# The first norm by products with diagonal matrices, products on zeros ahead of them, and small loads issued later

## The chip, the cores and the metric

The kernel runs on one core of a Trainium2 chip. The metric is the time of one execution on the device in microseconds (us), median of several runs. A profile of one execution gives what each engine did: TensorE (PE; its weight loads are PEld), VectorE (DVE), ScalarE (ACT), GpSimd (POOL) and SyncE (SP), and the DMA queues.

## The reference, cut to what matters

Three transformer-like blocks work on x, 256 tokens of 1024 features, in float32, with weights of some 176 MB in all. The change lies in the very first steps: the first norm and what it feeds.

```python
def rms_norm(x, g):
    xf = x.astype(jnp.float32)
    y = xf * lax.rsqrt(jnp.mean(xf * xf, axis=-1, keepdims=True) + EPS)
    return (y * g.astype(jnp.float32)).astype(x.dtype)
...
        h = rms_norm(x, norm_mix_pre[i])
        if i % N_MIXERS == 0:
            h = sliding_window_attention(h, attn_w_qkv[j], attn_b_qkv[j], attn_sinks[j],
                                         attn_w_o[j], attn_b_o[j])
...
    qkv = h @ w_qkv + b_qkv
```

## The kernel before

The program is written out by hand: each engine has one instruction stream, and semaphores order the streams. Nothing is rescheduled, so the order in the code is the order on the engine.

The weights come as 336 units of 128 x 1024 float32 (512 KB). SyncE loads them into a ring of six buffers (`raw`): the first six at once, behind x, and each later one when VectorE has made the low half of the unit six before it (`lo_done`). Every matrix product is done in three products of reduced precision: ScalarE copies a unit to its high half (`w_hi`, helper `hi_of`, L151), VectorE subtracts that from the unit for the low half (`w_lo`, `lo_of`, L156), and the activations are split likewise into `a_hi` and `a_lo` (both in the tensor `both`). `hi_to(act, n)` and `lo_to(dve, n)` bring the halves of all units up to n. TensorE then runs high by high, high by low and low by high (L173, L174, L175), eight feature tiles for a unit, 24 products in all.

The activations of the first matrix product are the normed x, with its features on the partitions. x has two tiles of 128 tokens (TT = 2) and eight of 128 features (KT = 8). In the kernel before:

- ScalarE issues the loads of the identity (`ident`, in the table `tab`) and of `cols` (per-feature constants, the gains of all norms among them), squares both tiles of x with a sum (L291), and takes the root for both at once (L296); VectorE computes the mean before it (L304) and the inverse after it (L309).
- VectorE multiplies x by the factor in four pieces of 128 x 512 (`scale_dve`, L320) into `ybuf`.
- TensorE transposes the 16 blocks of `ybuf` (`turn_pe`, L275), each pair of feature tiles signalled when its four blocks are done.
- ScalarE copies each transposed feature tile, times the gain, to the high half (`halves_act`, L332), VectorE makes the low half, times the gain too (`halves_dve`, L337). Both wait for `cols`. VectorE waits for high halves in pairs.
- ScalarE makes the high halves of weight units 0 and 1, and VectorE their low halves, before those of the activations.
- TensorE multiplies units 0 to 3 of the query and key projection (`qk1_pe`); for unit 0 it waits for each low half of the activations.
- Ahead of the transposes TensorE does six products of the identity with itself in three groups (`keep_warm`, L283): one when the identity is there, and one after the sum of each tile.

GpSimd sets `pad` to zero at the very beginning (L2262); the convolutions further on use it. `ps` is the accumulator memory, `st` small statistics, `arena` scratch.

Of the kernel before, what the change touches and what calls it, by code (L numbers as in the profile page):

```python
# [40 lines left out]

WARM_FIRST, WARM = 2, 4
HELD = 4
# [43 lines left out]
def build(nc, w, x_in, cols_in, misc_in, tables_in, rows_in, ws_in, wdt_in, out):  # L87
# [182 lines left out]
    def turn_pe(pe, q, base=4, tiles=range(KT)):  # L270
        for k in tiles:
            if k % 4 == 0:
                pe.wait_ge(q.scaled, 2 * TT * q.n + TT * (k // 4 + 1))
            for tt in range(TT):
                mm = pe.transpose(turned(k, base)[:, tt * P:(tt + 1) * P], ybuf[:, tt, k * P:(k + 1) * P], ident)  # L275
            if k % 2:
                mm.then_inc(q.turned, 1)

    def keep_warm(pe, products, bank, *after):

        pe.wait_ge(*after)
        for _ in range(products):
            pe.matmul(ps[:, bank, 0:P], ident, ident, start=True, stop=True)  # L283

# [9 lines left out]
    def norm_root(act, q, c0):  # L294
        act.wait_ge(q.mean, q.n + 1)
        act.activation(st[:, c0 + 4:c0 + 6], st[:, c0 + 2:c0 + 4], ACT.Sqrt).then_inc(q.root, 1)  # L296

    def norm_act(act, q, view, done, c0):
        norm_squares(act, q, view, done, c0)
        norm_root(act, q, c0)  # L300

# [5 lines left out]
    def norm_inverse(dve, q, c0):  # L307
        dve.wait_ge(q.root, q.n + 1)
        dve.reciprocal(st[:, c0 + 6:c0 + 8], st[:, c0 + 4:c0 + 6]).then_inc(q.inv, 1)  # L309
        dve.wait_ge(q.inv, q.n + 1)  # L310

    def norm_dve(dve, q, c0):
        norm_mean(dve, q, c0)
        norm_inverse(dve, q, c0)

# [1920 lines left out]
    with nc.Block() as block:  # L2236

        @block.sync
        def _(sp):
            for tt in range(TT):  # L2240
                sp.dma_start(x[:, tt, :], x_rows[:, tt, :]).then_inc(x_loaded[tt], 16)
            for s in range(RING):
# [49 lines left out]
        def _(act):  # L2292
            act.dma_start(ident, tables_in[:, T_ID:T_ID + P]).then_inc(ident_loaded, 16)
            act.dma_start(cols[:], cols_in).then_inc(cols_loaded, 16)
            act.preload_act_table(ACT.Sqrt)
            norm_act(act, first, lambda tt: x[:, tt, :], lambda tt: (x_loaded[tt], 16), 8)
            hi_to(act, 1)
            act.wait_ge(cols_loaded, 16)
            halves_act(act, first, 0)
            act.dma_start(tab[:, T_D1:T_D2], tables_in[:, T_D1:T_D2]).then_inc(early_loaded, 16)  # L2300
            act.dma_start(misc[:, 0:M_BS], misc_in[:, 0:M_BS].to_broadcast([P, M_BS])).then_inc(early_loaded, 16)
# [22 lines left out]
        def _(dve):  # L2324
            norm_dve(dve, first, 8)
            scale_dve(dve, first, 8, x)
            lo_to(dve, 1)
            dve.wait_ge(cols_loaded, 16)
            halves_dve(dve, first, 0)
            attn1_dve(dve)  # L2330
            dve.wait_ge(d_sem.w_hi, 1)
# [21 lines left out]
        @block.tensor  # L2353
        def _(pe):
            keep_warm(pe, WARM_FIRST, 7, ident_loaded, 16)
            for tt in range(TT):
                keep_warm(pe, WARM_FIRST, 7, first.sum, tt + 1)
            turn_pe(pe, first)
            attn1_pe(pe)

            ffn_pe(pe, ffn[0], N_FFN0, updates[0], updates[1])
            sgu_pe(pe, updates[1])
            ffn_pe(pe, ffn[1], N_FFN1, updates[2], updates[3])
            mixer_in_pe(pe, updates[3], at2)
            scan_pe(pe)
            attn2_pe(pe)
            mlp_pe(pe, updates[4], updates[5])
# [126 lines left out]
```

## Time and profile before

| | |
|---|---|
| median of 3 runs | 1078.44 us (1078.4 to 1078.48) |
| profiled execution | 1078.52 us |
| its span, first to last instruction | 1076.5 us |
| TensorE busy | 1057.4 us, 98% |
| VectorE busy | 820.3 us, 76% |
| ScalarE busy | 673.4 us, 63% |
| HBM read | 183.29 MB, 171 GB/s over the span |
| mean granted clock of TensorE | 0.998 |

The span is the part that the profile sees; 2.0 us of the execution lie around it. An engine that is busy 98% of the time leaves 19.1 us of idle time in all, and where it lies is read from stretches. The granted clock is a fraction of 2.4 GHz; 0.50 is 1.2 GHz.

### The profile page before, as it was taken

To read this page: it belongs to the slowest core of one execution; us is meant where nothing else is said; L and a number is where in the kernel's file an instruction comes from. 1 tells how busy PE (TensorE), PEld (TensorE's weight loads), DVE (VectorE), ACT (ScalarE), POOL (GpSimd) and SP (SyncE) were. 2 spreads that over 40 slices of the span, in tenths; PEclk is the share of its full clock that TensorE was granted. 3 is DMA by queue.
4 is the path that set the end of the run, shared out by engine and by line. 5 is a ranking of instruction groups with operands and counts; after the bars stand their busy time and mean duration, and the time that the engine had idled before them with its cause. 6 is when DMAs were issued, how large, how long until landed. Compare 5 with 4: busy or idle time off the path is not lost. (4 is left out here: it accounts for less than half of the span.)

```text
span 1076.5 us, 18647 instructions
## 1 busy us (share of the span) xinstructions
PE 1057.4 (98%) x6022; PEld 899.8 (84%) x6022; DVE 820.3 (76%) x1460; ACT 673.4 (63%) x1270; POOL 39.7 (4%) x71
## 2 busy tenths in 40 slices
PE   7999999999999999999999999999999999999997
PEld 7978888888788888888888888899678888888886
DVE  6777998888754678877998888798779748666664
ACT  6567565555765867666564555777777747455553
POOL 0010000000010002220000000000000000000000
PEclk9999999999999999999999999999999999999999
DMA  8463666556365565453666556265212545655541
GB/s 332 130 226 128 205 203 213 176 192 198 119 233 197 174 215 173 160 164 112 202 207 212 177 194 196 83 219 170 79 40 80 180 154 161 210 190 185 191 155 40
DMA packets 51380, 185.04 MB, mean 172 GB/s; under 512 B 5728, under 2 KB 6240, under 8 KB 51328
## 3 DMA queue, kind: packets, MB, share of 16 engines
q1 hardware_dynamic: 49248, 178.28, 49.6%
q0 software_dynamic: 1504, 5.44, 1.6%
q8 instruction: 31, 0.51, 0.2%
q10 hardware_dynamic: 576, 0.64, 0.2%
q14 instruction: 21, 0.17, 0.1%
HBM read 183.29 MB, written 1.05 MB: 171 GB/s over the span
## 5 line engine op out<-in xcount | busy, mean ns | idle before, releaser
L156 DVE TENSOR_TENSOR w_lo<-raw,w_hi 128x1024 fp32r<-128x1024 f32 x336 | 411.7, 1233 | 71.3 <-ACT w_hi L151 67.1
L151 ACT ACTIVATE w_hi<-raw 128x1024 fp32r<-128x1024 f32 x336 | 350.8, 1054 | 68.9 <-PE ps L253 43.1
L201 PE MATMUL ps<-both,w_hi 128*128 128x512 f32 x1104 | 358.7, 396 | 0.9 <-DVE arena L658 0.9
L253 PE MATMUL ps<-w_hi,both 128*128 128x512 f32 x992 | 291.5, 394 | 1.1 <-DVE both L2211 0.5
L199 PEld LDWEIGHTS ps<-both,w_lo 128*128 128x128 f32 x1104 | 207.4, 188 | 48.0
L199 PE MATMUL ps<-both,w_lo 128*128 128x256 f32 x1104 | 216.9, 278 | 0.0
L253 PEld LDWEIGHTS ps<-w_hi,both 128*128 128x128 f32 x992 | 183.4, 188 | 37.9 <-issue 1.2
L201 PEld LDWEIGHTS ps<-both,w_hi 128*128 128x128 f32 x1104 | 173.4, 189 | 4.2 <-DVE arena L658 1.7
L253 PE MATMUL ps<-w_lo,both 128*128 128x512 f32 x496 | 157.2, 390 | 0.0
L253 PEld LDWEIGHTS ps<-w_lo,both 128*128 128x128 f32 x496 | 93.1, 188 | 20.1
L623 ACT ACTIVATE arena<-arena 128x256 f32<-128x256 f32 x44 | 18.4, 419 | 100.3 <-DVE arena L654 100.3
L173 PE MATMUL ps<-both,w_hi 128*128 128x256 f32 x256 | 74.1, 290 | 1.2 <-DVE arena L426 0.7
L174 PE MATMUL ps<-both,w_hi 128*128 128x256 f32 x256 | 72.4, 283 | 0.0
L175 PE MATMUL ps<-both,w_lo 128*128 128x256 f32 x256 | 72.4, 283 | 0.0
L173 PE MATMUL ps<-w_hi,both 128*128 128x512 f32 (+1 forms) x160 | 61.2, 382 | 0.6 <-DVE both L462 0.6
L175 PE MATMUL ps<-w_hi,both 128*128 128x512 f32 (+1 forms) x160 | 59.0, 369 | 0.0
L174 PE MATMUL ps<-w_lo,both 128*128 128x512 f32 (+1 forms) x160 | 59.0, 369 | 0.0
L173 PEld LDWEIGHTS ps<-both,w_hi 128*128 128x128 f32 x256 | 48.9, 191 | 3.9 <-issue 2.0
L654 DVE SCALAR_TENSOR_TENSOR arena<-pad,cols,arena 128x256 f32<-128x256 f32 x88 | 42.6, 485 | 10.2 <-DVE arena L650 0.3
L174 PEld LDWEIGHTS ps<-both,w_hi 128*128 128x128 f32 x256 | 49.0, 192 | 0.2
L175 PEld LDWEIGHTS ps<-both,w_lo 128*128 128x128 f32 x256 | 49.0, 191 | 0.0
L2192 ACT ACTIVATE arena<-ps 128x256 f32<-128x256 f32 x32 | 12.2, 381 | 48.9 <-PE ps L201 48.9
(212 smaller groups left out, 1206.8 us busy)
## 6 DMA issues: line engine op xcount, KB each, us to landing
raw<-in_w SPq DMA_DIRECT2D x336, 512.0 KB, 3.4
row<-in_rows POOLq DMA_DIRECT2D x7, 512.0 KB, 4.0
x<-in_x SPq DMA_DIRECT2D x2, 512.0 KB, 4.3
out<-x SPq DMA_DIRECT2D x4, 256.0 KB, 2.0
misc<-in_misc POOLq DMA_DIRECT2D x1, 512.0 KB, 6.1
arena<-in_ws POOLq DMA_DIRECT2D x1, 512.0 KB, 9.2
tab<-in_tables POOLq DMA_DIRECT2D x1, 320.0 KB, 4.9
tab<-in_tables POOLq DMA_DIRECT2D x1, 256.0 KB, 5.3
```

The source lines that it names most:

```text
L151: act.activation(w_hi[:, s, :], raw[:, s, :], ACT.Copy).then_inc(hi_done, 1)
L156: dve.tensor_tensor(w_lo[:, s, :], raw[:, s, :], w_hi[:, s, :].bitcast(F32), ALU.subtract).then_inc(lo_done, 1)
L173: pe.matmul(o, l_hi, r_hi, start=first, stop=False)
L174: pe.matmul(o, l_hi, r_lo, start=False, stop=False)
L175: return pe.matmul(o, l_lo, r_hi, start=False, stop=last)
L199: mm = pe.matmul(ps[:, bank, 0:SEQ], w_lo[:, s, tile(k)], a_hi[:, k, :], start=False, stop=False)
L201: mm = pe.matmul(ps[:, bank, :].rearrange("p (h t) -> p h t", h=2), w_hi[:, s, tile(k)], both[:, :, k, :], start=k == 0, stop=k == KT - 1)
L253: mm = pe.matmul(ps[:, 2 * tt + c, :], a[:, slot, t], b[:, s, c * 512:(c + 1) * 512], start=f, stop=z)
L623: act.activation(F_GL[:, b, :], F_CV[:, b, :], ACT.Gelu_apprx_tanh).then_inc(f.gelu, 1)
L654: dve.scalar_tensor_tensor(F_CV[:, b, :], pad[:, b, k:k + SEQ], col(k), F_CV[:, b, :], ALU.mult, ALU.add).then_inc(f.conv, 1)
L2192: act.activation(M_PT[:, t % 3, :], ps[:, m_bank(t, i), SEQ:2 * SEQ], ACT.Copy).then_inc(m_sem.part, 1)
```

## The change

The first norm's factor is no longer applied by VectorE to x. Instead VectorE makes, for each token tile, a diagonal matrix of the factors (the identity times a column, 128 x 128, in `DIAGONAL` in the arena), and TensorE multiplies each block of x by it: `x_block.T @ diagonal` transposes and scales in one product. These are plain float32 products (L314) in the place of transposes. The statistics are done tile by tile, each with its own root and inverse (`first_act`, `first_dve`), the mean and the epsilon going into the root's scale and bias. The order of the blocks changes: all eight of tile 0 come first, then all eight of tile 1, and a pair is signalled when tile 1's are done.

The identity is loaded by SyncE between the two tiles of x. `cols` is issued by ScalarE after the square of tile 0. The products that `keep_warm` makes are on zeros (`pad`), ten from the moment that `pad` is set, and two more after the sum of tile 0.

Only unit 0's halves are made ahead of the activations' halves; unit 1's come after them, and the loads of a table and of `misc` behind unit 1's high half.

```diff
--- before.py
+++ after.py
@@ -39,7 +39,7 @@
 
 
 
-WARM_FIRST, WARM = 2, 4
+WARM_FIRST, WARM = 10, 2
 HELD = 4
 UNIT = 1024
 
@@ -270,7 +270,7 @@
     def turn_pe(pe, q, base=4, tiles=range(KT)):
         for k in tiles:
             if k % 4 == 0:
-                pe.wait_ge(q.scaled, 2 * TT * q.n + TT * (k // 4 + 1))
+                pe.wait_ge(q.scaled, TT * q.n + TT * (k // 4 + 1))
             for tt in range(TT):
                 mm = pe.transpose(turned(k, base)[:, tt * P:(tt + 1) * P], ybuf[:, tt, k * P:(k + 1) * P], ident)
             if k % 2:
@@ -280,7 +280,40 @@
 
         pe.wait_ge(*after)
         for _ in range(products):
-            pe.matmul(ps[:, bank, 0:P], ident, ident, start=True, stop=True)
+            pe.matmul(ps[:, bank, 0:P], pad[:, 0, 0:P], pad[:, 0, 0:P], start=True, stop=True)
+
+    DIAGONAL = cut(0, TT, P)
+
+    def first_act(act):
+
+        act.wait_ge(pad_ready, 2)
+        for tt in range(TT):
+            act.wait_ge(x_loaded[tt], 16)
+            act.activation(junk, x[:, tt, :], ACT.Square, accum_out=st[:, 8 + tt:9 + tt]).then_inc(first.sum, 1)
+            if tt == 0:
+                act.dma_start(cols[:], cols_in).then_inc(cols_loaded, 16)
+            act.wait_ge(first.sum, tt + 1)
+            act.activation(st[:, 12 + tt:13 + tt], st[:, 8 + tt:9 + tt], ACT.Sqrt, bias=EPS_COL,
+                           scale=1.0 / D).then_inc(first.root, 1)
+
+    def first_dve(dve):
+
+        dve.wait_ge(ident_loaded, 16)
+        for tt in range(TT):
+            dve.wait_ge(first.root, tt + 1)
+            dve.reciprocal(st[:, 14 + tt:15 + tt], st[:, 12 + tt:13 + tt]).then_inc(first.inv, 1)
+            dve.wait_ge(first.inv, tt + 1)
+            dve.tensor_scalar(DIAGONAL[:, tt, :], ident, st[:, 14 + tt:15 + tt], None, ALU.mult).then_inc(first.scaled, 1)
+
+    def first_pe(pe):
+
+        for tt in range(TT):
+            pe.wait_ge(x_loaded[tt], 16)
+            pe.wait_ge(first.scaled, tt + 1)
+            for k in range(KT):
+                mm = pe.matmul(turned(k)[:, tile(tt)], x[:, tt, tile(k)], DIAGONAL[:, tt, :], start=True, stop=True)
+                if tt == TT - 1 and k % 2:
+                    mm.then_inc(first.turned, 1)
 
     def norm_squares(act, q, view, done, c0, scratch=junk):
 
@@ -292,12 +325,8 @@
                            accum_out=st[:, c0 + tt:c0 + tt + 1]).then_inc(q.sum, 1)
 
     def norm_root(act, q, c0):
-        act.wait_ge(q.mean, q.n + 1)
+        act.wait_ge(q.mean, q.n)
         act.activation(st[:, c0 + 4:c0 + 6], st[:, c0 + 2:c0 + 4], ACT.Sqrt).then_inc(q.root, 1)
-
-    def norm_act(act, q, view, done, c0):
-        norm_squares(act, q, view, done, c0)
-        norm_root(act, q, c0)
 
     def norm_mean(dve, q, c0):
         dve.wait_ge(q.sum, TT * (q.n + 1))
@@ -305,13 +334,9 @@
                           ALU.mult, ALU.add).then_inc(q.mean, 1)
 
     def norm_inverse(dve, q, c0):
-        dve.wait_ge(q.root, q.n + 1)
+        dve.wait_ge(q.root, TT * q.n + 1)
         dve.reciprocal(st[:, c0 + 6:c0 + 8], st[:, c0 + 4:c0 + 6]).then_inc(q.inv, 1)
-        dve.wait_ge(q.inv, q.n + 1)
-
-    def norm_dve(dve, q, c0):
-        norm_mean(dve, q, c0)
-        norm_inverse(dve, q, c0)
+        dve.wait_ge(q.inv, TT * q.n + 1)
 
     def scale_dve(dve, q, c0, src, halves=range(2)):
         for h in halves:
@@ -2237,8 +2262,9 @@
 
         @block.sync
         def _(sp):
-            for tt in range(TT):
-                sp.dma_start(x[:, tt, :], x_rows[:, tt, :]).then_inc(x_loaded[tt], 16)
+            sp.dma_start(x[:, 0, :], x_rows[:, 0, :]).then_inc(x_loaded[0], 16)
+            sp.dma_start(ident, tables_in[:, T_ID:T_ID + P]).then_inc(ident_loaded, 16)
+            sp.dma_start(x[:, 1, :], x_rows[:, 1, :]).then_inc(x_loaded[1], 16)
             for s in range(RING):
                 sp.dma_start(raw[:, s, :], w[s]).then_inc(raw_loaded[s], 16)
             with sp.Fori(0, UNITS // RING - 1) as i:
@@ -2290,13 +2316,12 @@
 
         @block.scalar
         def _(act):
-            act.dma_start(ident, tables_in[:, T_ID:T_ID + P]).then_inc(ident_loaded, 16)
-            act.dma_start(cols[:], cols_in).then_inc(cols_loaded, 16)
             act.preload_act_table(ACT.Sqrt)
-            norm_act(act, first, lambda tt: x[:, tt, :], lambda tt: (x_loaded[tt], 16), 8)
-            hi_to(act, 1)
+            first_act(act)
+            hi_to(act, 0)
             act.wait_ge(cols_loaded, 16)
             halves_act(act, first, 0)
+            hi_to(act, 1)
             act.dma_start(tab[:, T_D1:T_D2], tables_in[:, T_D1:T_D2]).then_inc(early_loaded, 16)
             act.dma_start(misc[:, 0:M_BS], misc_in[:, 0:M_BS].to_broadcast([P, M_BS])).then_inc(early_loaded, 16)
             hi_to(act, 5)
@@ -2322,11 +2347,11 @@
 
         @block.vector
         def _(dve):
-            norm_dve(dve, first, 8)
-            scale_dve(dve, first, 8, x)
-            lo_to(dve, 1)
+            first_dve(dve)
+            lo_to(dve, 0)
             dve.wait_ge(cols_loaded, 16)
             halves_dve(dve, first, 0)
+            lo_to(dve, 1)
             attn1_dve(dve)
             dve.wait_ge(d_sem.w_hi, 1)
             dve.tensor_tensor(wdt_lo[:], wdt[:], wdt_hi[:].bitcast(F32), ALU.subtract).then_inc(d_sem.w_lo, 1)
@@ -2352,10 +2377,9 @@
 
         @block.tensor
         def _(pe):
-            keep_warm(pe, WARM_FIRST, 7, ident_loaded, 16)
-            for tt in range(TT):
-                keep_warm(pe, WARM_FIRST, 7, first.sum, tt + 1)
-            turn_pe(pe, first)
+            keep_warm(pe, WARM_FIRST, 7, pad_ready, 1)
+            keep_warm(pe, WARM, 7, first.sum, 1)
+            first_pe(pe)
             attn1_pe(pe)
 
             ffn_pe(pe, ffn[0], N_FFN0, updates[0], updates[1])
```

On ScalarE, at the beginning of the program, before the change: the two small loads stand ahead of everything, and two weight units (L151) ahead of the activations' high halves (L332, the rows with pre_turned).

```order
L2293 DMA tab<-in_tables 128x128
L2294 DMA cols<-in_cols 128x370
L2295 ACT_TABLE_LOAD
L291 ACTIVATE arena,st<-x 128x1024 [waits x_loaded0]
L291 ACTIVATE arena,st<-x 128x1024 [waits pre_sum,x_loaded1]
L296 ACTIVATE st<-st 128x2 [waits pre_mean]
L151 ACTIVATE w_hi<-raw 128x1024 [waits raw_loaded0]
L151 ACTIVATE w_hi<-raw 128x1024 [waits raw_loaded1]
L332 ACTIVATE both<-ps,cols 128x256 [waits pre_turned,cols_loaded]
L332 ACTIVATE both<-ps,cols 128x256 [waits pre_turned] x7
L2300 DMA tab<-in_tables 128x384
L2301 DMA misc<-in_misc 128x368
```

The same place of ScalarE with the change:

```order
L2319 ACT_TABLE_LOAD
L292 ACTIVATE arena,st<-x 128x1024 [waits x_loaded0,pad_ready]
L294 DMA cols<-in_cols 128x370
L296 ACTIVATE st<-st 128x1 [waits pre_sum]
L292 ACTIVATE arena,st<-x 128x1024 [waits x_loaded1]
L296 ACTIVATE st<-st 128x1 [waits pre_sum]
L151 ACTIVATE w_hi<-raw 128x1024 [waits raw_loaded0]
L357 ACTIVATE both<-ps,cols 128x256 [waits pre_turned,cols_loaded]
L357 ACTIVATE both<-ps,cols 128x256 [waits pre_turned] x7
L151 ACTIVATE w_hi<-raw 128x1024 [waits raw_loaded1]
L2325 DMA tab<-in_tables 128x384
L2326 DMA misc<-in_misc 128x368
```

The load of `cols` now stands behind the wait for x tile 0, and the high half of unit 1 behind the eight high halves of the activations.

On VectorE, at the beginning of the program, before the change:

```order
L304 TENSOR_SCALAR st<-st 128x2 [waits pre_sum]
L309 RECIPROCAL st<-st 128x2 [waits pre_root]
L320 TENSOR_SCALAR arena<-x,st 128x512 [waits pre_inv]
L320 TENSOR_SCALAR arena<-x,st 128x512 x3
L156 TENSOR_TENSOR w_lo<-raw,w_hi 128x1024 [waits hi_done] x2
L337 SCALAR_TENSOR_TENSOR both<-ps,cols,both 128x256 [waits pre_hi,cols_loaded]
L337 SCALAR_TENSOR_TENSOR both<-ps,cols,both 128x256 [waits pre_hi] x7
```

And with the change (L306 makes a diagonal matrix, L362 is the activations' low half):

```order
L304 RECIPROCAL st<-st 128x1 [waits pre_root,ident_loaded]
L306 TENSOR_SCALAR arena<-tab,st 128x128 [waits pre_inv]
L304 RECIPROCAL st<-st 128x1 [waits pre_root]
L306 TENSOR_SCALAR arena<-tab,st 128x128 [waits pre_inv]
L156 TENSOR_TENSOR w_lo<-raw,w_hi 128x1024 [waits hi_done]
L362 SCALAR_TENSOR_TENSOR both<-ps,cols,both 128x256 [waits pre_hi,cols_loaded]
L362 SCALAR_TENSOR_TENSOR both<-ps,cols,both 128x256 [waits pre_hi] x7
L156 TENSOR_TENSOR w_lo<-raw,w_hi 128x1024 [waits hi_done] x5
```

The four wide scalings have become two of 128 columns, and one low half of a weight unit (L156) has moved from ahead of the activations' low halves to behind them.

## Rows read from the trace of the kernel before

**Rows 1.** Table of windows: length, busy PE, PEld, DVE, ACT, POOL, clock, DMA, GB/s.

```profile
12.50:112.00 99.50, 99.41 (x745) 87.84 (x746) 77.03 (x183) 67.42 (x159) 7.76 (x10) 1.00 0.56 187
112.00:1071.00 959.00, 951.27 (x5251) 806.11 (x5249) 736.26 (x1265) 596.76 (x1096) 31.14 (x55) 1.00 0.51 169
```

**Rows 2.** Timeline of ScalarE from 0: start us, us, engine, line, operation.

```profile
4.38 1.06 ACT L291 ACTIVATE arena<-x 128x1024 f32<-128x1024 f32 x1 [1.42 <-DMA x<-in_x]
6.21 1.06 ACT L291 ACTIVATE arena<-x 128x1024 f32<-128x1024 f32 x1 [0.67 <-DMA x<-in_x]
...
10.18 2.47 ACT L332 ACTIVATE both<-ps,cols 128x256 fp32r<-128x256 f32 x6 [0.27 <-PE ps L275]
...
11.81 0.84 ACT L332 ACTIVATE both<-ps,cols 128x256 fp32r<-128x256 f32 x2
```

**Rows 3.** Timeline of GpSimd and VectorE from 0.

```profile
0.75 0.53 POOL L2262 MEMSET pad<- 128x520 f32 x1 [0.29 <-POOLq L2449]
...
8.03 1.67 DVE L320 TENSOR_SCALAR arena<-x,st 128x512 f32<-128x512 f32 x4
9.62 2.35 DVE L156 TENSOR_TENSOR w_lo<-raw,w_hi 128x1024 fp32r<-128x1024 f32 x2
...
11.89 3.22 DVE L337 SCALAR_TENSOR_TENSOR both<-ps,cols,both 128x256 fp32r<-128x256 f32 x8
...
15.02 2.35 DVE L156 TENSOR_TENSOR w_lo<-raw,w_hi 128x1024 fp32r<-128x1024 f32 x2
```

**Rows 4.** Timeline of TensorE from 0.

```profile
4.59 2.22 PE L283 MATMUL ps<-tab 128*128 128x128 f32 x8 [4.59 <-DMA tab<-in_tables]
7.41 1.23 PE L283 MATMUL ps<-tab 128*128 128x128 f32 x4 [0.60 <-ACT arena L291]
8.96 3.25 PE L275 MATMUL ps<-tab,arena 128*128 128x128 f32 x16 [0.33 <-DVE arena L320]
12.51 0.36 PE L173 MATMUL ps<-both,w_hi 128*128 128x256 f32 x1 [0.30 <-DVE both L337]
...
15.63 0.28 PE L173 MATMUL ps<-both,w_hi 128*128 128x256 f32 x1
```

**Rows 5.** Timeline of SyncE: the issues of the first six weight units.

```profile
1.68 3.09 SPq L2243 DMA_DIRECT2D raw<-in_w  x6
```

**Rows 6.** Landing times from the issue: weights of L2243, then the identity.

```profile
DMA to landing us min/median/max: 5.9/7.8/9.6
...
tab<-in_tables ACTq DMA_DIRECT2D x1, 64.0 KB, 3.8
```

**Rows 7.** Timeline of TensorE in narrow windows: records one behind another.

```profile
5.96 0.85 PE L283 MATMUL ps<-tab 128*128 128x128 f32 x3
...
103.79 0.60 PE L419 MATMUL ps<-tab,st 128*128 128x128 f32 x4
...
16.71 0.28 PE L173 MATMUL ps<-both,w_hi 128*128 128x256 f32 x1
```

**Rows 8.** The transposes, line 275, of 11 to 12: durations ns min/median/max, starts.

```profile
L275 PE MATMUL ps<-tab,arena x8: 272/355/421, 10.7 to 11.9; 128*128 128x128 f32 x8
```

**Rows 9.** A ScalarE load behind weights: issues, their landing times, queues of 13.3 to 14.5.

```profile
12.14 0.34 SPq L2247 DMA_DIRECT2D raw<-in_w  x1
12.26 0.33 ACTq L2300 DMA_DIRECT2D tab<-in_tables  x1
...
raw<-in_w SPq DMA_DIRECT2D x1, 512.0 KB, 5.0
tab<-in_tables ACTq DMA_DIRECT2D x1, 192.0 KB, 4.7
...
q1 hardware_dynamic: 128, 0.46, 100.3%
```

**Rows 10.** Table of windows at the kernel's end, columns as in rows 1.

```profile
1070.00:1071.00 1.00, 0.99 (x5) 0.49 (x3) 0.51 (x1) 0.00 (x0) 0.00 (x0) 1.00 1.04 387
...
1073.00:1074.00 1.00, 0.00 (x0) 0.00 (x0) 1.00 (x2) 0.00 (x0) 0.00 (x0) 0.59 0.00 0
```

## The prediction

> **What bounds the kernel now.** I first read the table of windows, to see where TensorE waits at all [rows 1]. From 12.5 us to 112 it is busy in 99.4 of 99.5 us, and from there to its end near 1071 in 951.3 of 959. The change touches nothing behind 20 us, so an early shift should be carried whole to the end. Before 12.5 us TensorE had all else to wait for the first norm: of its 1057.4 us 6.7 lie there. That prologue is all that is at stake. My landmark in it is the first product of weight unit 1, at 15.63 us [rows 4]: behind it TensorE starts a product every 0.12 us: the tenth starts at 16.71 [rows 7].
>
> The prologue's chain stands in the timelines of ScalarE, VectorE and TensorE [rows 2 to 4]. x tile 0 is there at 4.38, tile 1 at 6.21; the square (1.06), the reading of the sum, mean, root and inverse follow, and at 8.03 VectorE scales x, four pieces in 1.67. The first transpose starts at 8.96, the first high half at 10.18; the second is done near 11.0. But VectorE makes the low halves of weight units 0 and 1 first (9.62 to 11.97), so its first low half of the activations starts only at 11.89. TensorE starts unit 0 at 12.51 and goes at VectorE's pace: the next thing on VectorE starts 3.13 after the first of the eight low halves (15.02).
>
> **The change, part by part.** The sum has one disputed term, the landing of `cols` (the gains by which both engines scale every half); first what stands around it.
>
> *Loads.* The first weight unit lands 5.9 us after its issue at 1.68, the sixth 9.6 after its issue at 4.3, thus at 7.6 and 13.9: one unit in 1.27 us [rows 5, 6] (the issues stand 3.09/6 = 0.52 apart, so the sixth starts at 4.3). Without the 64 KB identity and the 185 KB of `cols` at its side x tile 0 comes earlier by some 0.2, at 4.2 (64 KB at that rate are 0.16; bounds zero and 0.4). Tile 1 stands behind the identity: 4.2 + 0.2 + 1.27 = 5.65, against 6.21. Units 0 to 4 would follow at 6.9, 8.2, 9.5, 10.7 and 12.0 if nothing shares with them.
>
> *Statistics.* Tile 1: square from 5.65, sum at 6.85, root to 7.05, inverse to 7.25, then a scaling of 128 columns where there were four of 512. The nearest row is 1.67/4 = 0.42 for 512; 128 cost between 0.1 and 0.42, I take 0.2 [rows 3]: tile 1's diagonal is ready at 7.5, tile 0's near 6.0. The mean's instruction goes; a second root and inverse, 0.2 each, lie under the wait for tile 1.
>
> *TensorE.* A plain product of 128 columns leaves two records (6 products, 8 + 4 records), a transpose one [rows 4]. So 16 products make 32 records where 16 stood. A record costs 0.213 at the slow clock ((0.85 - 0.42)/2) and 0.108 at the fast one ((0.60 - 0.275)/3) [rows 7]. The clock's level shows in the transposes: 421 ns each at the slow one, 272 at the end, the median of the last eight 355, so the rise from 1.2 to 2.4 GHz came near 11.6, 7.0 us after TensorE's first product, with 0.6 and 0.3 of idle time between [rows 4, 8]. Ten products on zeros now start near 1.35, when the pad is set (GpSimd's 0.53 from 0.75) [rows 3], and last 0.16 + 20 x 0.213 = 4.4 at the slow clock, to 5.8; two more last to 6.7, which is 0.7 behind tile 0's diagonal. If the clock rises by 6, tile 0's products take 16 x 0.108 = 1.75, the first pair of tile 1 is through at 8.5 and all at 9.7. If it again rises near 11.6, the pair ends at 6.7 + 20 x 0.213 + 0.2 = 11.1. These are the two bounds; I give the early rise two in three.
>
> *VectorE.* Only unit 0's low half now stands ahead of the activations; unit 1's follows all eight. Unit 0: high half 7.1 to 8.2, low half to 9.4, ahead of what needs them.
>
> *`cols`.* It is issued behind the first square, near 4.2, where it stood ahead of everything. By then SyncE has issued both tiles, the identity and units 0 to 3 (at 0.52 each, unit 3 near 3.7, unit 4 near 4.3). What becomes of a small ScalarE load behind such a queue? The trace has one: the 192 KB table of distances, issued at 12.26 just behind a weight unit (12.14, landing 5.0 later, at 17.1). It landed 4.7 later, at 17.0, with that unit; from 13.3 to 14.5 its queue q10 moved not one packet, while q1 alone filled the engines (100.3%) [rows 9]. The identity, issued at 0.75 with no queue ahead, took 3.8 [rows 6]. Read so, `cols` lands with unit 3: 10.7 and 0.6 for its packets and unit 4's between them, 11.3. Bounds: 10.9 (sharp with unit 3) and 12.0 (with unit 4).
>
> The Trainium skill says otherwise (DMA: Bandwidth & Descriptors, "Issuing engines are not separate DMA queues"): loads issued from several engines run on the same 16 DMA engines and interleave. By that `cols` would land near 8 us and the result would be that of the first rival below. The table of distances, 4.7 us to its landing with no packet in 1.2 of them, does not agree with it [rows 9].
>
> *The sum.* From `cols` at 11.3: two high halves 0.84 [rows 2] (the second starts 0.36 behind), 0.05 to VectorE, 3.13 until it is free for unit 1, 1.21 for it, and 0.15 to TensorE (the eight low halves take 3.22 at 0.39 each, so the first ends at 11.89 + 0.47, against TensorE's 12.51): 5.38. Unit 1 starts at 16.68 against 15.63, 1.0 later. Queued behind ScalarE's wait for `cols` are unit 1's high half (11.3 + 8 x 0.36 + 1.06 = 15.3, just when VectorE asks), and the loads of the table and `misc`, first needed beyond 20 us; behind VectorE's, the low halves of units 1 to 5, needed 24 x 0.12 = 2.9 apart and made 1.14 apart (2.35 - 1.21). TensorE begins unit 0 at 12.8, not 12.51. SyncE fetches unit 7 when unit 1's low half is done, at 16.5 instead of 12.0; TensorE needs it six units behind unit 1, beyond 32. The profiled execution took 1078.52 for its span of 1076.5, 0.08 above the median of the runs, 1078.44. Forecast: 1078.44 + 1.04 = **1079.5 us**, within 0.2% (2.2 us, about what a measurement of this kernel tells from no change). `cols` decides between gain and loss at 15.63 - 5.38, some 10.3 us.
>
> **The rivals.**
> *The loads interleave and the prologue shortens.* For it: x tile 1 came 1.83 behind tile 0 and not 1.27, so the two small loads did share with x in the first 6 us; against it: no queue stood ahead of them then. `cols` is there near 8.3, unit 0, slowed by its packets, at 7.3; high half to 8.4, low half to 9.6, unit 1 at 9.6 + 3.13 + 1.21 + 0.15 = 14.1: 1.5 gained, 1076.9. With a late clock the pair at 11.1 governs: 11.1 + 5.38 = 16.5, 0.9 lost, 1079.3.
> *The clock falls in the new gap: slower by over 0.2%.* If the clock rises early, TensorE is through at 9.7 and stands until 12.8, 3.1 us. At the kernel's end it stops at 1071.0, and the granted clock is 0.59 in the mean of 1073 to 1074: 0.18 of that microsecond at 1.00, the rest at 0.50, so the fall came at 1073.2, 2.2 us after the last product [rows 10]. Against it: the trace has no other gap beyond 1 us, so how surely a gap of 3.1 brings a fall is not to be read. Then unit 0 runs for 24 x 0.213 = 5.1 from 12.8 to 17.9, 2.3 behind, and each record of unit 1 costs 0.09 more until the clock rises again, 0 to 0.8: 1080.7 to 1081.5, middle 1081.1. It decides where the gap passes 2 to 3 us.
> *The zeros do nothing for the clock.* Under the wait for `cols` that is hidden (11.1 against 11.3): the forecast stays, and no gap opens.
>
> **How the numbers follow.** `cols` late and the clock kept: 0.40, 1079.1 to 1080.2 by the bounds of its landing. Late and the clock fallen: 0.27, 1081.1. Interleaved with an early clock: 0.22, 1076.9, 0.4 to either side; with a late clock 0.07, 1078 to 1079.3. What I have not seen: 0.04. A range for 8 in 10 reaches from one side to the other: 1076.7 to 1081.3. Slower by over 0.2% is the fallen clock, 0.28; faster by over 0.2% wants 0.6 more than the rival gives, 0.03; between, 0.69.
>
> **What would show it.** ScalarE's first high half (L357): near 11.3, released by `cols`, or near 8.5, released by TensorE. The landing of `cols`: some 7 us from its issue, or 4. TensorE's records of L314, 0.213 or 0.108 apart, show the clock; those of L173 to L175 in unit 0, whether it fell (0.213 apart, not threes every 0.39). Unit 1's first product: 16.7. I am wrong if `cols` comes before 10.3, or if TensorE has a gap beyond 20 us that it did not have.

## The result, and the profile after

The changed kernel takes 1079.93 us (median of 20 runs, 1079.5 to 1080.55) against 1078.46 (median of 20, 1078.25 to 1078.73): a ratio of 1.0013, 95% interval 1.0007 to 1.0019. It is slower by 1.5 us, within the 0.2% that the prediction took for no change. The profiled execution took 1079.53 for a span of 1077.7.

The table of windows of the changed kernel, columns as in [rows 1]:

```profile
12.50:112.00 99.50, 98.75 (x740) 87.14 (x741) 77.36 (x183) 68.16 (x161) 8.02 (x10) 1.00 0.55 189
112.00:1071.00 959.00, 951.17 (x5252) 806.43 (x5251) 736.12 (x1266) 597.67 (x1098) 31.21 (x55) 1.00 0.51 168
```

The rest of the kernel is as busy as it was; 0.66 us of the loss shows in the first window (99.41 there before). Timeline of ScalarE, which answers to [rows 2]:

```profile
4.15 1.06 ACT L292 ACTIVATE arena<-x 128x1024 f32<-128x1024 f32 x1 [2.12 <-DMA x<-in_x]
4.20 0.39 ACTq L294 DMA_DIRECT2D cols<-in_cols  x1
...
7.54 1.06 ACT L292 ACTIVATE arena<-x 128x1024 f32<-128x1024 f32 x1 [1.92 <-DMA x<-in_x]
...
11.06 0.84 ACT L357 ACTIVATE both<-ps,cols 128x256 fp32r<-128x256 f32 x2 [1.09 <-DMA cols<-in_cols]
```

Landing times from the issue, of `cols` (L294) and of x tile 1 (L2267, issued at 1.68):

```profile
DMA to landing us min/median/max: 6.8/6.8/6.8
...
DMA to landing us min/median/max: 5.8/5.8/5.8
```

`cols` lands at 11.0, and ScalarE, done with its other work 1.09 earlier, waits for that. x tile 1 comes at 7.5, later than the 6.21 of before. VectorE, as in [rows 3]:

```profile
9.25 0.29 DVE L306 TENSOR_SCALAR arena<-tab,st 128x128 f32<-128x128 f32 x1
10.00 1.23 DVE L156 TENSOR_TENSOR w_lo<-raw,w_hi 128x1024 fp32r<-128x1024 f32 x1 [0.46 <-ACT w_hi L151]
12.02 3.23 DVE L362 SCALAR_TENSOR_TENSOR both<-ps,cols,both 128x256 fp32r<-128x256 f32 x8 [0.79 <-ACT both L357]
15.16 2.35 DVE L156 TENSOR_TENSOR w_lo<-raw,w_hi 128x1024 fp32r<-128x1024 f32 x2
```

And TensorE, as in [rows 4]:

```profile
1.33 5.25 PE L283 MATMUL ps<-pad 128*128 128x128 f32 x24 [1.33 <-POOL st L2289]
6.42 1.98 PE L314 MATMUL ps<-arena,x 128*128 128x128 f32 x16
9.69 2.02 PE L314 MATMUL ps<-arena,x 128*128 128x128 f32 x16 [1.30 <-DVE arena L306]
12.64 0.36 PE L173 MATMUL ps<-both,w_hi 128*128 128x256 f32 x1 [0.93 <-DVE both L362]
...
16.43 0.39 PE L173 MATMUL ps<-both,w_hi 128*128 128x256 f32 x1 [0.51 <-DVE w_lo L156]
```

Unit 1's first product stands at 16.43, 0.80 behind the 15.63 of before. TensorE's last product, though, starts 1.19 behind (1071.79 against 1070.60). The other 0.39 arose far from the change. Timeline of VectorE near 800 us, of the kernel before:

```profile
797.77 0.69 DVE L1900 TENSOR_TENSOR arena<-ps,ex 128x512 f32<-128x512 f32 x1 [0.40 <-PE ps L1774]
798.57 0.69 DVE L1906 TENSOR_TENSOR arena<-arena,ps 128x512 f32<-128x512 f32 x1
```

and the same two instructions of the changed kernel:

```profile
798.63 0.69 DVE L1925 TENSOR_TENSOR arena<-ps,ex 128x512 f32<-128x512 f32 x1 [0.41 <-PE ps L1799]
799.79 0.69 DVE L1931 TENSOR_TENSOR arena<-arena,ps 128x512 f32<-128x512 f32 x1 [0.47 <-DVE arena L1925]
```

The second starts 0.80 behind the first before, and 1.16 behind it after. The 16 small products that wait for a VectorE instruction further behind it (L1917) then take 2.22 us instead of 1.89. Timelines of TensorE, before:

```profile
800.34 1.89 PE L1757 MATMUL ps<-arena 128*128 128x64 f32 x16
```

and after:

```profile
801.19 2.22 PE L1782 MATMUL ps<-arena 128*128 128x64 f32 x16
```

So the profiled execution lost 0.80 in the prologue and 0.39 behind it, and 0.2 less lies around its span (1.8 instead of 2.0): 1.0 in all, at the lower end of its runs.

### The profile page after: what moved, and what is told of

Its sections match the earlier page's. It is cut to its first block and busy times, and to the rows that moved or that the text cites. A ratio compares the mean times of both kernels' runs of the same rounds, so it can differ in the third digit from the quotient of the medians.

```text
span 1077.7 us, 18705 instructions
## 1 busy us (share of the span) xinstructions
PE 1060.2 (98%) x6050; PEld 902.9 (84%) x6050; DVE 819.0 (76%) x1458; ACT 673.5 (62%) x1271; POOL 40.0 (4%) x71
## 3 DMA queue, kind: packets, MB, share of 16 engines
HBM read 183.29 MB, written 1.05 MB: 171 GB/s over the span
## 5 line engine op out<-in xcount | busy, mean ns | idle before, releaser
L156 DVE TENSOR_TENSOR w_lo<-raw,w_hi 128x1024 fp32r<-128x1024 f32 x336 | 409.3, 1226 | 71.9 <-ACT w_hi L151 67.7
L151 ACT ACTIVATE w_hi<-raw 128x1024 fp32r<-128x1024 f32 x336 | 350.8, 1054 | 68.1 <-PE ps L253 43.1
L679 DVE SCALAR_TENSOR_TENSOR arena<-pad,cols,arena 128x256 f32<-128x256 f32 x88 | 42.6, 484 | 10.2 <-DVE arena L675 0.3
L2217 ACT ACTIVATE arena<-ps 128x256 f32<-128x256 f32 x32 | 12.2, 382 | 48.9 <-PE ps L201 48.9
```

What stands on the lines that cost most here:

```text
L151: act.activation(w_hi[:, s, :], raw[:, s, :], ACT.Copy).then_inc(hi_done, 1)
L156: dve.tensor_tensor(w_lo[:, s, :], raw[:, s, :], w_hi[:, s, :].bitcast(F32), ALU.subtract).then_inc(lo_done, 1)
L679: dve.scalar_tensor_tensor(F_CV[:, b, :], pad[:, b, k:k + SEQ], col(k), F_CV[:, b, :], ALU.mult, ALU.add).then_inc(f.conv, 1)
L2217: act.activation(M_PT[:, t % 3, :], ps[:, m_bank(t, i), SEQ:2 * SEQ], ACT.Copy).then_inc(m_sem.part, 1)
```

## The experiments

Each kernel was timed beside the kernel before (its medians 1078.51, 1078.54 and 1078.55 in three groups; the row "before" is the first measurement, beside the changed kernel). "Remainder" is the time from unit 1's first product to the start of the last; "wait" is VectorE's idle time ahead of the instruction near 800 us. All but the column of medians are from one profiled execution of each kernel, which can lie off its median: no_zeros was profiled at 1079.94, after_pad at 1079.15.

| kernel | median (lowest to highest) | first high half | unit 1 | last product | remainder | wait |
|---|---|---|---|---|---|---|
| before | 1078.46 (1078.25 to 1078.73) | 10.18 | 15.63 | 1070.60 | 1054.97 | none |
| after | 1079.93 (1079.5 to 1080.55) | 11.06 | 16.43 | 1071.79 | 1055.36 | 0.47 |
| cols_first | 1078.49 (1078.35 to 1080.29) | 9.88 | 15.25 | 1070.57 | 1055.32 | 0.47 |
| ident_act | 1079.56 (1078.9 to 1080.22) | 11.18 | 16.54 | 1071.84 | 1055.30 | 0.47 |
| both_act | 1077.76 (1077.58 to 1078.03) | 9.21 | 14.57 | 1069.88 | 1055.31 | 0.47 |
| ident_behind | 1079.96 (1079.43 to 1081.96) | 10.92 | 16.29 | 1071.61 | 1055.32 | 0.47 |
| both_pad | 1077.49 (1077.27 to 1077.6) | 9.41 | 14.78 | 1069.85 | 1055.07 | none |
| no_zeros | 1079.21 (1079.01 to 1079.99) | 11.56 | 16.93 | 1072.24 | 1055.31 | 0.47 |
| before_cols_late | 1078.61 (1077.91 to 1079.02) | 11.23 | 15.94 | 1070.82 | 1054.88 | none |
| cols_sp | 1077.95 (1077.7 to 1078.18) | 9.40 | 14.93 | 1070.15 | 1055.22 | 0.47 |
| before_zeros | 1078.47 (1078.26 to 1078.68) | 9.86 | 15.63 | 1070.59 | 1054.96 | none |
| after_pad | 1079.57 (1079.04 to 1080.21) | 10.88 | 16.25 | 1071.21 | 1054.96 | none |
| after_order | 1079.64 (1079.39 to 1080.79) | 11.76 | 16.76 | 1071.92 | 1055.16 | 0.47 |
| both_order | 1077.84 (1077.79 to 1078.01) | 9.97 | 14.98 | 1070.29 | 1055.31 | 0.47 |

**The two small loads.** The theory: the late `cols` is what the change loses by. The rival: the identity in SyncE's row, which delays x. Each is put back alone, then both.

cols_first, `cols` at the start of ScalarE's stream:

```diff
-            if tt == 0:
-                act.dma_start(cols[:], cols_in).then_inc(cols_loaded, 16)
...
+            act.dma_start(cols[:], cols_in).then_inc(cols_loaded, 16)
             act.preload_act_table(ACT.Sqrt)
```

> The changed kernel, but the load of cols is issued at the very beginning by ScalarE, as before; the identity stays with SyncE between the two tiles of x. Theory A (in the changed kernel two things are late and cols, which lands at 11.0, is the later by 0.7: tile 1 of x lands at 7.5, so that the first pair of products on it ends near 10.4): cols lands near 6.5, the first high half starts at 10.3 to 10.5, released by TensorE, unit 1 starts at 15.7 to 15.8, the time is 0.6 to 0.8 us below the changed kernel, near 1079.2. Theory B (cols alone; tile 1's late landing is an accident of one execution, or is caused by the load of cols itself): tile 1 lands near 5.7, unit 1 starts near 14.3, the time is near 1077.

Measured: 1078.49, ratio 1.0001 (0.9992 to 1.001). Unit 1 starts at 15.25, between the places that the two theories give it. x tile 0 came at 5.10 instead of 4.15; `cols` was under way beside it (issued at 0.75, landed 4.5 later). Timeline of ScalarE:

```profile
5.10 1.06 ACT L292 ACTIVATE arena<-x 128x1024 f32<-128x1024 f32 x1 [2.61 <-DMA x<-in_x]
...
9.88 1.57 ACT L355 ACTIVATE both<-ps,cols 128x256 fp32r<-128x256 f32 x4 [0.93 <-PE ps L312]
```

The halves are released by TensorE and no longer by `cols`: by the medians 1.44 us of the loss go with this one line.

ident_act, the identity alone back at the start of ScalarE's stream:

```diff
-            sp.dma_start(ident, tables_in[:, T_ID:T_ID + P]).then_inc(ident_loaded, 16)
...
+            act.dma_start(ident, tables_in[:, T_ID:T_ID + P]).then_inc(ident_loaded, 16)
             act.preload_act_table(ACT.Sqrt)
```

> The changed kernel, but the identity is issued at the very beginning by ScalarE, as before; cols stays behind the first square. Theory A: tile 1 lands at 5.5 to 6.0 instead of 7.5, TensorE is through with the norm by 10, but cols still lands near 11, so unit 1 starts at 16.3 to 16.5 and the time stays that of the changed kernel, 1079.9, within 0.3. Theory C (tile 1's landing is what costs): 1 us or more below the changed kernel. If the clock falls in the longer gap ahead of unit 0, the time is 1 to 2 us above it.

Measured: 1079.56, ratio 1.001 (1.0001 to 1.0019). Everything but `cols` is ready earlier. Timeline of ScalarE:

```profile
5.98 1.04 ACT L292 ACTIVATE arena<-x 128x1024 f32<-128x1024 f32 x1
...
11.18 0.47 ACT L357 ACTIVATE both<-ps,cols 128x256 fp32r<-128x256 f32 x1 [2.44 <-DMA cols<-in_cols]
```

ScalarE now stands 2.44 us for `cols` and unit 1 is at 16.54. By the medians the identity's place alone is worth 0.37 while `cols` is late, less than either kernel's runs spread.

both_act, both edits together:

> The changed kernel, but the identity and cols are both issued at the very beginning by ScalarE, as in the kernel before; all the rest of the change stays. Theory A: tile 1 lands near 6.1, cols near 6.6, the first high half starts near 8.9, unit 1 at 14.2 to 14.5, the time is 1077.0 to 1077.4, 1.1 to 1.4 below the kernel before. If the order of the halves or the 32 records are what costs, it is not below the kernel before, 1078.4.

Measured: 1077.76, ratio 0.9993 (0.9984 to 1.0002). Unit 1 starts at 14.57, 1.06 ahead of before. With `cols` early the identity's place is worth 0.73 (against cols_first). Timeline of VectorE, then of TensorE:

```profile
8.61 1.23 DVE L156 TENSOR_TENSOR w_lo<-raw,w_hi 128x1024 fp32r<-128x1024 f32 x1 [0.55 <-ACT w_hi L151]
10.16 3.23 DVE L360 SCALAR_TENSOR_TENSOR both<-ps,cols,both 128x256 fp32r<-128x256 f32 x8 [0.33 <-ACT both L355]
13.31 4.62 DVE L156 TENSOR_TENSOR w_lo<-raw,w_hi 128x1024 fp32r<-128x1024 f32 x4
```

```profile
6.64 3.81 PE L312 MATMUL ps<-arena,x 128*128 128x128 f32 x32 [0.30 <-DVE arena L304]
10.79 0.36 PE L173 MATMUL ps<-both,w_hi 128*128 128x256 f32 x1 [0.34 <-DVE both L360]
```

ident_behind, the identity in SyncE's row behind both tiles of x:

```diff
             sp.dma_start(x[:, 0, :], x_rows[:, 0, :]).then_inc(x_loaded[0], 16)
-            sp.dma_start(ident, tables_in[:, T_ID:T_ID + P]).then_inc(ident_loaded, 16)
             sp.dma_start(x[:, 1, :], x_rows[:, 1, :]).then_inc(x_loaded[1], 16)
+            sp.dma_start(ident, tables_in[:, T_ID:T_ID + P]).then_inc(ident_loaded, 16)
```

> The changed kernel, but SyncE issues the identity behind both tiles of x instead of between them. If the identity's 128 rows of 512 B slow the transfers queued behind them (tile 1 took 5.8 us from its issue in the changed kernel, 5.0 before), tile 1 now lands near 5.6 and the first weight unit is the slow one; if the slow stretch of the DMA engines from 3.5 to 6.0 has another cause, tile 1 is again slow. Either way cols lands near 11 and the time stays at 1079.9 within 0.3.

Measured: 1079.96, ratio 1.0017 (1.0008 to 1.0026). Tile 1 came at 5.68 instead of 7.54, and unit 1 only 0.14 earlier, since `cols` (10.92) still decided. So the late tile 1 of the changed kernel was hidden.

cols_sp, the identity on ScalarE and `cols` in SyncE's row behind x, ahead of the weights:

```diff
             sp.dma_start(x[:, 1, :], x_rows[:, 1, :]).then_inc(x_loaded[1], 16)
+            sp.dma_start(cols[:], cols_in).then_inc(cols_loaded, 16)
```

> The changed kernel with the identity issued by ScalarE at the start and cols in SyncE's row right behind x tile 1, ahead of the weights. Theory A: what delays cols is only the loads issued ahead of it: it lands by 8, the first half starts by 9, the low halves near 9.7, unit 1 at 14.1 to 14.5: 1077.3 to 1077.8. Theory B: its short rows slow SyncE's row as the identity's did in the changed kernel, and the weights of unit 0 or 1 come late: cols by 8 but unit 1 not before 15, 1078.3 or more.

Measured: 1077.95, ratio 0.9995 (0.9986 to 1.0004). In between: `cols` landed 4.8 after its issue at 1.68, no half waited for it, but unit 0's weights came later. Timeline of ScalarE:

```profile
8.29 1.06 ACT L151 ACTIVATE w_hi<-raw 128x1024 fp32r<-128x1024 f32 x1 [0.83 <-DMA raw<-in_w]
9.40 0.84 ACT L355 ACTIVATE both<-ps,cols 128x256 fp32r<-128x256 f32 x2
```

That `cols` was late by the loads issued ahead of it holds on another engine's queue too.

before_cols_late, the kernel before with `cols` issued behind tile 0's square:

```diff
+            if q is first and tt == 0:
+                act.dma_start(cols[:], cols_in).then_inc(cols_loaded, 16)
...
-            act.dma_start(cols[:], cols_in).then_inc(cols_loaded, 16)
```

> The kernel before with one edit: the load of cols is issued by ScalarE behind tile 0's square instead of at the start. Theory A: cols lands near 11 us here too, but its first reader on VectorE is queued behind the low halves of the units, which take VectorE until 11.97, so that nothing waits: 1078.5, within 0.2. Theory B: the late landing costs what it costs in the changed kernel, about 1 us: 1079.5.

Measured: 1078.61, ratio 1.0 (0.999 to 1.0009). Theory A holds for the time; its mechanism was too simple. `cols` again took 6.8 and came at 11.2. Without `cols` beside it x tile 1 came at 5.63 instead of 6.21, so VectorE had the weights' low halves done at 11.45 instead of 11.97, and the activations' low halves then waited, to 12.20 instead of 11.89: unit 1 stood 0.31 later. In the old order the same late load costs 0.1 by the medians and 0.3 in the profile; in the new one 1.4 to 1.8 (medians of the pairs above). There the low halves could start at 10.2 (both_act); in the old order VectorE's other work holds them until 11.5 to 11.9.

**The zeros.** no_zeros is both_act with the count cut:

```diff
-WARM_FIRST, WARM = 10, 2
+WARM_FIRST, WARM = 1, 2
```

> The same kernel with both small loads at the start, with the number of zero matmuls cut to one (width two in the second place), so TensorE idles until tile 0's transposes. Theory A: the zeros are what raises the granted clock ahead of the transposes; without them it rises near 10 to 11 us, the transposes stand 0.21 us apart instead of 0.13, the first half starts near 10.6 instead of 9.2, unit 0 and unit 1 1.0 to 1.4 us later: near 1079. Theory B: the zeros do nothing for the end, since the diagonals and low halves on VectorE order the start: 1077.76, within 0.2.

Measured: 1079.21, ratio 1.0008 (0.9999 to 1.0017), 1.45 above both_act, so theory A. The profiled execution lies at the slow end of its runs (1079.94), so unit 1 stands 2.36 behind both_act's in it. Timeline of TensorE in two narrow windows:

```profile
7.63 2.77 PE L312 MATMUL ps<-arena,x 128*128 128x128 f32 x12
...
11.25 1.53 PE L312 MATMUL ps<-arena,x 128*128 128x128 f32 x11
```

From 7.63 on the records start 0.21 apart (the level of 1.2 GHz). The last eleven start at this spacing too at first; from 11.62 on they start 0.11 apart, as the 32 of both_act do (3.81 in all, 2.4 GHz). TensorE had been idle from 2.1 to 5.8.

before_zeros gives the zeros to the kernel before, with nothing else:

```diff
-            pe.matmul(ps[:, bank, 0:P], ident, ident, start=True, stop=True)
+            pe.matmul(ps[:, bank, 0:P], pad[:, 0, 0:P], pad[:, 0, 0:P], start=True, stop=True)
...
-            keep_warm(pe, WARM_FIRST, 7, ident_loaded, 16)
+            keep_warm(pe, WARM_FIRST, 7, pad_ready, 1)
```

(with the counts of the changed kernel, and a wait for the identity ahead of the transposes)

> The kernel before with the zero products alone: the same number of products on zeros from the beginning as in the changed kernel, instead of products of the identity. Theory A: the clock is at its upper level when the transposes begin near 9, which then take some 2.2 us instead of 3.7, but the low halves on VectorE begin only behind both units' low halves of the weights at 11.9, so the time stays: 1078.5, within 0.2. Theory B: the zeros are what the best changed kernel gains by (removing them there cost 1.45): 1077.1 to 1077.6 here.

Measured: 1078.47, ratio 0.9999 (0.999 to 1.0008): theory A. Timeline of VectorE, then of TensorE:

```profile
9.62 2.36 DVE L156 TENSOR_TENSOR w_lo<-raw,w_hi 128x1024 fp32r<-128x1024 f32 x2
11.89 3.23 DVE L337 SCALAR_TENSOR_TENSOR both<-ps,cols,both 128x256 fp32r<-128x256 f32 x8
```

```profile
9.07 1.94 PE L275 MATMUL ps<-tab,arena 128*128 128x128 f32 x16 [0.94 <-DVE arena L320]
12.52 0.35 PE L173 MATMUL ps<-both,w_hi 128*128 128x256 f32 x1 [1.52 <-DVE both L337]
```

The transposes take 1.94 instead of 3.25 [rows 4], and TensorE waits the difference: VectorE decides the start.

**The order of unit 1's halves.** In both_order and after_order unit 1's halves stand ahead of the activations' again:

```diff
-            hi_to(act, 0)
+            hi_to(act, 1)
...
-            lo_to(dve, 0)
+            lo_to(dve, 1)
```

(and the same calls behind the halves fall away)

> The same edit in the kernel with both small loads issued by ScalarE at the start (1077.76, low halves from 10.16, unit 1 at 14.57). Theory A: here VectorE has no idle time to put unit 1's low half into, it pushes the low halves back by about 1 and takes the wait of 0.8 ahead of unit 1 away: 1077.8, within 0.3, so that the order is worth something only together with the late loads. Theory B: the order of before is better in itself by half a us: 1077.2 to 1077.3.

Measured: 1077.84, ratio 0.9993 (0.9984 to 1.0002), against 1077.76: theory A. The low halves start at 11.24 instead of 10.16, and unit 1 at 14.98 instead of 14.57; the two medians can't be told apart.

> The changed kernel with one part undone: unit 1's high and low halves stand ahead of the halves of the first projection again, as before. Theory A: with cols landing at 11.0 VectorE has the time for unit 1's low half ahead of its wait, and unit 1 no longer waits for it behind 3.2 us of other work: unit 0 within 0.4 of 12.64, unit 1 at 15.8 to 16.0 instead of 16.43: 1079.3 to 1079.5. Theory B: unit 1's low half only pushes the low halves back by as much as it saves: 1079.9.

Measured: 1079.64, ratio 1.0011 (1.0002 to 1.002), between the two theories, and the profiled execution doesn't decide: `cols` took 7.2 in it, and unit 1's weights came late, so that VectorE was through with the low halves only at 13.1. Timeline of VectorE:

```profile
11.88 1.23 DVE L156 TENSOR_TENSOR w_lo<-raw,w_hi 128x1024 fp32r<-128x1024 f32 x1 [0.34 <-ACT w_hi L151]
13.02 3.22 DVE L362 SCALAR_TENSOR_TENSOR both<-ps,cols,both 128x256 fp32r<-128x256 f32 x8
```

**The wait near 800 us.** The changed prologue has one VectorE instruction fewer, waits for semaphores counted. both_pad is both_act, and after_pad the changed kernel, with one small instruction more that writes an unused column:

```diff
+            dve.memset(st[:, 94:95], 0.0)
             first_dve(dve)
```

> The kernel with both small loads issued by ScalarE at the start and the rest of the change (1077.76), and one small memset more on VectorE ahead of everything, so that every later VectorE instruction stands one place further in its engine's stream. Theory A: the 0.35 us that all changed kernels lose near 800 us (VectorE starts a TENSOR_TENSOR 0.43 us after its semaphore was there, and 16 matmuls take 2.22 instead of 1.89) comes from where that instruction stands in VectorE's stream; the wait is gone with one place more: 1077.4, and 1054.96 from unit 1's first product to TensorE's last. Theory B: it has to do with the matmuls or the time of the transfers: 1077.76 again, and 1055.3 between the same two.

Measured: 1077.49, ratio 0.999 (0.9981 to 0.9999), 1.05 us below the kernel before and the fastest of all.

> The changed kernel with one small memset more on VectorE ahead of everything. Theory A: the loss near 800 us comes with the place of an instruction in VectorE's stream: no wait of 0.47 us there, 1055.0 from unit 1's first product to TensorE's last instead of 1055.36, and 1079.6. Theory B: the two did not go together in the kernel with both small loads at the start by more than chance: 1079.9.

Measured: 1079.57, ratio 1.001 (1.0001 to 1.0019); the remainder is 1054.96, as before. By the medians after_pad is 0.36 faster than the changed kernel, but the two kernels' runs overlap widely (1079.04 to 1080.21, 1079.5 to 1080.55); it is the profile that shows the effect here. In both_pad the medians show it too: its runs end at 1077.6, and those of both_act begin at 1077.58. Timeline of VectorE in after_pad:

```profile
798.39 0.69 DVE L1925 TENSOR_TENSOR arena<-ps,ex 128x512 f32<-128x512 f32 x1 [0.40 <-PE ps L1799]
799.18 0.69 DVE L1931 TENSOR_TENSOR arena<-arena,ps 128x512 f32<-128x512 f32 x1
```

One instruction at 0.8 us takes the wait at 799 us away. The profile's page counts two VectorE instructions fewer in the changed kernel (1458 against 1460), but it leaves out waits for semaphores, and the changed kernel has one of those more (for the identity): 2257 in all against 2258. In the 14 kernels the wait is there exactly where VectorE's stream has 2257. The remainder is 1055.16 to 1055.36 in those nine and 1054.88 to 1055.07 in the other five, so it also varies by 0.2 for reasons that no run separates.

## Why the prediction was right, and where not

- **`cols`.** Predicted: landing at 11.3, 7.1 from its issue, with weight unit 3 (the units count from 0). Measured: 11.0, 6.8. The forecast rested on this time, and it was right; the reason given for it was not. Landing times from the issue of units 1, 2 and 3, issued at 2.62, 3.09 and 3.58:

```profile
raw<-in_w SPq DMA_DIRECT2D x1, 512.0 KB, 7.8
...
raw<-in_w SPq DMA_DIRECT2D x1, 512.0 KB, 8.8
...
raw<-in_w SPq DMA_DIRECT2D x1, 512.0 KB, 9.6
```

  Unit 1 landed at 10.4, unit 2 at 11.9 and unit 3 at 13.2, not at the predicted 10.7. So `cols` came ahead of units 2 and 3, which had been issued before it; with unit 3, as the rule said, it would have come at 13.2 or later. In ident_act, before_cols_late, ident_behind and after_pad it came behind unit 2 (at 10.6 to 10.8) and ahead of unit 3 (at 12.0 to 12.2). That two errors, a weight row 2.5 later than reckoned and a `cols` that did not stay behind it, met at 11 us is luck. What its queue (q10) did stands in the queue rows of the changed kernel, of 4.6 to 8.0 and then of 8.0 to 10.4 (packets, MB, share of the 16 engines):

```profile
q1 hardware_dynamic: 283, 1.05, 91.7%
...
q1 hardware_dynamic: 218, 0.77, 79.2%
q10 hardware_dynamic: 141, 0.19, 21.7%
```

  From its issue at 4.2 to 8.0 q10 moved nothing (from 3.5 to 6.0 the queue rows have q1 alone, too), as the table of distances did for a time in [rows 9]. Then it moved its 0.19 MB beside units 1 and 2. What ended the standstill no run shows. The Trainium skill (DMA: Bandwidth & Descriptors, "Issuing engines are not separate DMA queues") has such loads interleave. Here a load that came first did share (both_act: 5.3 to its landing beside x and the weights). One issued behind both tiles and five or six weight units stood for 3.8 us and shared only then (6.8 to its landing here and in before_cols_late, 6.5 in ident_act).
- **The chain behind it** was right, 5.38 from `cols` to unit 1: 16.43 - 11.06 = 5.37, and 5.36 to 5.37 in both_act, ident_act, cols_first and after_pad too. So unit 1 stood 0.25 ahead of the predicted 16.68, by the 0.24 that `cols` came earlier.
- **x tile 1** was predicted at 5.65 and came at 7.54: the step that the identity takes 0.2 of the row's time is wrong here, and with it the times of the weights behind it (unit 0 at 8.8 instead of 6.9). The 16 engines were not full while it stood there. Packets of the changed kernel from 3.5 to 6.0, then of both_act in the same window:

```profile
DMA packets 213, 0.50 MB, mean 199 GB/s; under 512 B 24, under 2 KB 101, under 8 KB 213
```

```profile
DMA packets 405, 0.97 MB, mean 389 GB/s; under 512 B 55, under 2 KB 218, under 8 KB 405
```

  Half the rate. With the identity on ScalarE's queue it did not happen (401 GB/s in ident_act), and with it behind tile 1 (ident_behind, 284) tile 1 was in time. But in cols_first the identity stood between the tiles too, with `cols` on ScalarE's queue from the start, and the rate was 410. The low rates come where the identity stood in SyncE's row and ScalarE's queue was empty until 4.2: 199 here, 246 in after_order (tile 1 at 7.86), 296 in after_pad (6.19), 284 in ident_behind. Which of the two conditions makes them, and why their size varies so, stays open. The late tile 1 was off the path here only because `cols` was later still.
- **The clock.** The early rise, given two in three, came, at 6.2: seven records are under way from 5 to 6 us and ten from 6 to 7, and tile 0's eight products, 16 records, take 1.98, where the 16 transposes of before took 3.25. Windows of the changed kernel:

```profile
5.00:6.00 1.00, 1.00 (x7) 1.00 (x7) 0.23 (x2) 0.60 (x3) 0.00 (x0) 1.00 0.76 193
6.00:7.00 1.00, 1.00 (x10) 1.00 (x9) 0.22 (x1) 0.00 (x0) 0.00 (x0) 1.00 1.05 397
```

  The records start 0.21 apart until 6.19 and 0.11 apart from there. The clock's column reads 1.00 in both rows and can't tell the level here: it does so over no_zeros' 21 slow records from 6.8 to 11.0 as well. The price of 0.108 a record was a little low: it was 0.12 (1.98/16).
- **The rival of the fallen clock** (0.27) did not come. The gap predicted as 3.1 was two, 1.30 and 0.93, because tile 1 was late. Where it was longest, in ident_act, TensorE stood 2.14 us ahead of 12.76, and unit 0 still went at the upper level: 24 records in 3.27 of busy time. The predicted 3.1 never came about, so that gap stays untested. Windows of ident_act, the gap, unit 0, and the kernel's end:

```profile
10.50:12.70 2.20, 0.12 (x2) 0.00 (x0) 0.57 (x2) 1.52 (x5) 0.00 (x0) 1.00 1.03 410
12.70:16.50 3.80, 3.27 (x24) 3.10 (x24) 3.80 (x9) 3.80 (x8) 0.00 (x0) 1.00 0.78 291
...
1077.00:1078.00 1.00, 0.00 (x0) 0.00 (x0) 0.00 (x0) 0.00 (x0) 0.00 (x0) 0.59 0.00 0
```

  There the fall came at 1077.2 (0.18 of the last window at full), 5.0 behind the end of the last product at 1072.2. In after_order it came 5.1 behind, in the changed kernel 2.4, in after_pad and ident_behind 2.0. The 2.2 read from [rows 10] was one draw of something that varies between 2.0 and 5.1, and no threshold for the rival.
- **The rival of the interleaved loads** put unit 1 at 14.1 and the time at 1076.9. both_act brings it about with early loads: 14.57 and 1077.76. Its direction was right, its size 0.9 too large, 0.35 of it the wait at 800 us.
- **"An early shift should be carried whole to the end"** is the other step that failed. The shift in the prologue was 0.80, but the remainder grew by 0.39 (profiled); one VectorE instruction more takes 0.27 away by the medians of both_act and both_pad. The median of 1079.93 lies inside the 1079.1 to 1080.2 given for a late `cols` with the clock kept, and 0.43 above the forecast. That the forecast of 1079.5 met the profiled 1079.53 is luck: the prologue cost 0.24 less than said, and the wait was not in the sum.
- The median lies 0.4 above the profiled execution. The kernels with a late `cols` spread over 1.05 to 2.5 us between their runs, both_act, both_pad, both_order and cols_sp over 0.2 to 0.5 (cols_first over 0.3, but for one run). no_zeros, with an early `cols` and a late rise of the clock, spreads over 1.0. It is likely that the landing varies so, and in no_zeros the rise of the clock, but only profiled executions show it, and this was not tested.

What stays open: why the one place in VectorE's stream decides over 0.47 us near 800. The trace shows where it happens, if waits for semaphores are counted as instructions. In the nine kernels with 2257 the pause stands behind the 1778th, a wait for a semaphore of 0.02 us; in the other five the 1778th is a wide instruction of 0.69 us (L1900 of before), which would cover a pause of that length. And in all 14 one packet of 8 KB of a queue that carries instructions (q14) comes when VectorE has started 1781 of them (1782 in ident_behind). Queue rows of the changed kernel, of 795 to 802:

```profile
q14 instruction: 1, 0.01, 0.4%
```

The Trainium skill (Runtime: NRT & Kernel Launch, "Instruction fetch mechanics") says that instructions are fetched in blocks whose crossing is mostly hidden, and that a taken branch out of the window stalls. A pause that stays at one count of instructions, with such a packet just behind it, fits a crossing that is not hidden. But the packet comes 0.67 us after the paused instruction has started (800.46 against 799.79), so it is not what that one waited for, and the cause is not shown.

## What to carry to other kernels

A small load costs by when it is issued, not only by its size: behind a burst of large ones 185 KB issued 3.0 us later landed 4.5 us later (both_act 1.2 and 6.5, the changed kernel 4.2 and 11.0), so issue what the prologue's chain needs before the bulk, and ask whose wait it will be. Keeping TensorE busy early pays where the chain goes through it (1.45 us here), and nothing where VectorE orders the start (before_zeros). And when an edit changes the number of instructions, compare the remainder of the kernel between two landmarks: a few tenths can come or go a long way from the edit, and one instruction more may take them back.

## What had not been expected

- `cols`, issued behind both tiles of x and five weight units, moved no packet for 3.8 us and then landed ahead of units 2 and 3.
- The rate of the loads from 3.5 to 6 us was 199 to 296 GB/s in the four kernels in which SyncE issued the identity and nothing came from ScalarE's queue until 4.2, against 351 to 410 in the other ten.
- TensorE's clock stayed at its upper level over a gap of 2.1 us, and at the end of an execution fell between 2.0 and 5.1 us after the last product.
- One VectorE instruction more at the beginning took a wait near 800 us away in two kernels, and made one of them faster by 0.27 us.
